# Half-by-half down and output projections, and staggered retention chunks, in a one-core decoder layer kernel

## The reference

```python
def _macaron_layer(x, mixer, f1g, f1u, f1d, ln1g, ln1b, ln2g, ln2b, f2g, f2u, f2d, ln3g, ln3b):
    x = _layernorm(ALPHA * x + 0.5 * _swiglu(x, f1g, f1u, f1d), ln1g, ln1b)
    m, st = mixer(x)
    x = _layernorm(ALPHA * x + m, ln2g, ln2b)
    x = _layernorm(ALPHA * x + 0.5 * _swiglu(x, f2g, f2u, f2d), ln3g, ln3b)
    return x, st
```

```python
    inner = jnp.einsum('bnhd,bmhd->bhnm', q, k) * decay[None]
    intra = jnp.einsum('bhnm,bmhe->bnhe', inner, v)
    cross = jnp.einsum('bnhd,bhde->bnhe', q, sp) * xi[None, :, :, None]
    s_new = jnp.exp(L * lg)[None, :, None, None] * sp + jnp.einsum('bmhd,bmhe->bhde', k * zeta[None, :, :, None], v)
```

## Time and profile before

| what | value |
|---|---|
| median of 3 runs | 1487.87 us (1487.46 to 1488.2) |
| the profiled execution's own time | 1489.0 us |
| its span, first to last instruction | 1487.3 us |
| mean granted TensorE clock | 0.972 of full |
| TensorE busy | 1405.3 us (94% of the span) |
| VectorE, ScalarE, GpSimd busy | 556.1, 417.2, 193.6 us |
| HBM read, written | 169.00 MB, 7.02 MB |

### The profile page before, as it was taken

The page is one execution under the profiler, slowest core; times in us unless marked ns, Lnnn a source line. Parts: engine busy times, 40 slices in busy tenths (PEclk is TensorE's granted clock), DMA queues, the critical chain, the costliest instruction groups (busy, mean ns, idle before and its releaser), DMA issues. The chain is left out here.

```text
span 1487.3 us, 27099 instructions
## 1 busy us (share of the span) xinstructions
PE 1405.3 (94%) x10150; PEld 1216.6 (82%) x10150; DVE 556.1 (37%) x1102; ACT 417.2 (28%) x622; POOL 193.6 (13%) x309
## 2 busy tenths in 40 slices
PE   6999999999999999999997768999899999999995
PEld 6999999999987647777773445567699999999994
DVE  3332323322251338893112446452533333322224
ACT  4333333212241231100131001340734343322223
POOL 0000000033213102212113212102500000000011
PEclk9999999999999989999998978999999999999998
DMA  5222222233322328888365744501022222223221
GB/s 190 84 86 84 85 85 84 68 115 106 94 67 75 103 73 261 261 267 265 133 220 188 244 149 170 194 6 57 29 85 85 85 86 93 89 68 90 87 80 60
DMA packets 65352, 176.76 MB, mean 119 GB/s; under 512 B 9681, under 2 KB 13778, under 8 KB 65042
## 3 DMA queue, kind: packets, MB, share of 16 engines
q1 hardware_dynamic: 49874, 131.30, 27.1%
q0 software_dynamic: 14560, 40.96, 8.4%
q10 hardware_dynamic: 864, 3.80, 0.7%
HBM read 169.00 MB, written 7.02 MB: 118 GB/s over the span
## 5 line engine op out<-in xcount | busy, mean ns | idle before, releaser
L365 PE MATMUL ps<-x_high,w_high 128*128 128x280 f32 (+1 forms) x1408 | 413.9, 294 | 17.8 <-DVE x_low L1078 10.6
L365 PE MATMUL ps<-x_high,w_low 128*128 128x280 f32 (+1 forms) x1408 | 411.0, 292 | 0.0
L365 PE MATMUL ps<-x_low,w_high 128*128 128x280 f32 (+1 forms) x1408 | 410.9, 292 | 0.0
L1072 DVE TENSOR_TENSOR w_low<-wring,w_high 128x1024 fp32r<-128x1024 f32 (+1 forms) x136 | 163.0, 1199 | 508.5 <-ACT w_high L839 508.4
L365 PEld LDWEIGHTS ps<-x_high,w_high 128*128 128x128 f32 x1408 | 267.9, 190 | 22.8 <-issue 13.6
L365 PEld LDWEIGHTS ps<-x_low,w_high 128*128 128x128 f32 x1408 | 268.0, 190 | 0.0
L365 PEld LDWEIGHTS ps<-x_high,w_low 128*128 128x128 f32 x1408 | 267.4, 190 | 0.0
L365 PE MATMUL ps<-xbuf,wring 128*128 128x280 f32 x1056 | 262.6, 405 | 1.2 <-ACT aux L839 0.9
L839 ACT ACTIVATE w_high<-wring 128x1024 fp32r<-128x1024 f32 (+1 forms) x136 | 140.7, 1035 | 423.7 <-PE ps L365 422.7
L365 PEld LDWEIGHTS ps<-xbuf,wring 128*128 128x128 f32 x1056 | 197.5, 191 | 58.3 <-issue 9.2
L365 PE MATMUL ps<-h_high,w_low 128*128 128x280 f32 (+1 forms) x704 | 203.8, 289 | 0.0
(11 more groups left out here) (190 smaller groups left out, 1184.5 us busy)
## 6 DMA issues: line engine op xcount, KB each, us to landing
wring<-in_wg SPq DMA_DIRECT2D x44, 512.0 KB, 3.4
wring<-in_wu SPq DMA_DIRECT2D x44, 512.0 KB, 3.4
wring<-in_w_in SPq DMA_DIRECT2D x33, 512.0 KB, 4.1
wring<-in_wd SPq DMA_DIRECT2D x32, 512.0 KB, 3.5
dring<-in_k_pool POOLq DMA_DIRECT2D x64, 256.0 KB, 4.5
dring<-in_k_pool SPq DMA_DIRECT2D x64, 256.0 KB, 3.9
dring<-in_v_pool POOLq DMA_DIRECT2D x64, 256.0 KB, 4.3
dring<-in_v_pool SPq DMA_DIRECT2D x64, 256.0 KB, 3.9
```

Of the source, the lines that this page charges most:

```text
L365: return nc.tensor.matmul(out, lhs, rhs, start=start, stop=stop, **kw)
L1072: v.tensor_tensor(wl[:, to, 0:n], w4[:, s, 0:n], wh[:, to, 0:n].bitcast(F32), ALU.subtract) \
```

## The change

1. The down projections of both SwiGLUs run over all 8 output tiles for column half 0, and then once more over all 8 for half 1. The weights of the down projection are loaded and split twice. Half 0's norm is spread over the second pass; half 1's norm comes in the next stage (for n = 0 between the first tiles of the input projection) or at the end (n = 2). For half 0 of n = 0 and 2 POOL makes the whole sum of the tiles and the sum of the squares, so that TensorE has one matmul for each; half 1 is as before, with ScalarE's squares.
2. The output projection goes the same way, half 0 for all tiles and then half 1, and the second SwiGLU's first tile takes turns with norm 1 of half 1. VectorE writes the full value (`gained`), ScalarE only the rounded one.
3. Retention: the inner products of chunk t + 1 are made ahead of the turned output of chunk t - 1, and the output bank alternates between 2 and 6.
4. The sample states' decay goes to POOL, and the stores of the new states behind all eight of these.
5. The loads of `cst` and `acc` move, to behind ScalarE's x_high and to POOL behind norm 0.

```diff
-FF_W = [FT // 2 + KT] * 3 + [FT // 2]
+FF_W = [FT // 2 + 2 * KT] * 3 + [FT // 2]
...
+        def summed(n, a):
+
+            return n != 1 and a == 0
...
-                for s in range(3):
-                    down_chunk(s, wds[m][0])
-                with loop(sp, KT - 1, [(f, 1) for f in free[:3]]) as i:
-                    for s in range(3):
-                        down_chunk(s, wds[m][bass.ds(i + 1, 1)].rearrange("a p n -> (a p) n"))
+                for a in range(2):
+                    with loop(sp, KT, [(f, 1) for f in free[:3]]) as i:
+                        for s in range(3):
+                            down_chunk(s, wds[m][bass.ds(i, 1)].rearrange("a p n -> (a p) n"))
...
+                def down(a, j):
+                    pe.wait_ge(sem("r_done"), rdone.up())
+                    for s in range(3):
+                        if s == 2:
+                            pe.wait_ge(sem("hl_done"), FT * (m + 1))
+                        pe.wait_ge(sem("wl_done"), wl_done.up())
+                        wide_split(m, j, (j + s) % 2, hh, hl, 8 * s, DOWN[s] // P, FT, parts=(a,)).then_inc(sem(f"w_free{s}"), 1)
+
                 with loop(pe, KT // 2, [(wl_done, 6), (rdone, 2)]):
                     for j in range(2):
-                        pe.wait_ge(sem("r_done"), rdone.up())
...
-                norm(2 * m)
...
+                        down(0, j)
+                down(1, 0)
+                norm_mean(2 * m, 0)
+                down(1, 1)
+                down(1, 0)
+                down(1, 1)
+                norm_var(2 * m, 0)
+                with loop(pe, KT // 4, [(wl_done, 6), (rdone, 2)]):
+                    for j in range(2):
+                        down(1, j)
+
+            def norm_mean(n, a):
+                m = int(n > 0)
                 if n == 0:
                     pe.wait_ge(sem("cst_in"), 16)
-                pe.wait_ge(sem("sum_done"), (KT - 2) * (n + 1))
+                pe.wait_ge(sem("sum_done"), sum_at(2 * n + a + 1))
+                last = mm(ps[:, 4 + a, 0:HW[m]], c("mean"), rsum_t[:, cols(a, m)], True, summed(n, a))
+                if not summed(n, a):
+                    pe.wait_ge(sem("r_done"), 2 + KT * (2 * n + a + 1))
+                    last = mm(ps[:, 4 + a, 0:HW[m]], c("mean"), rs[n][:, KT - 1, cols(a, m)], False, True)
+                last.then_inc(sem("mean_full"), 1)
+
+            def norm_var(n, a):
...
+                if summed(n, a):
+                    pe.wait_ge(sem("sq_done"), sq_at(2 * n) + 1)
+                    mm(ps[:, 6 + a, 0:HW[m]], c("mean"), squares(3, m)).then_inc(sem("sq_free"), 1)
+                    return
...
@@ -461,6 +501,10 @@
                     if a:
                         last.then_inc(sem(f"w_free{t}"), 1)
+                    elif t == 0:
+                        norm_mean(0, 1)
+                    elif t == 1:
+                        norm_var(0, 1)
...
+            ret_in(real(0), P)
             for t in TILES:
-                ret_in(real(t), P)
                 value_pages(1)
                 pe.wait_ge(sem("it_done"), t + 1)
                 pe.wait_ge(sem("qx_done"), t + 1)
                 pe.wait_ge(sem("sr_done"), t + 1)
                 for hd in range(RH):
-                    o = ps[:, 2, hd * P:(hd + 1) * P]
+                    o = ps[:, 2 + 4 * (t % 2), hd * P:(hd + 1) * P]
...
                 new_state(t + 1, P, vr[:, t, :])
-                value_pages(1)
-                ret_out(t)
-                pe.wait_ge(sem("mixr_done"), t + 1)
+                if t < 3:
+                    ret_in(real(t + 1), P)
+                    value_pages(1)
+                if t:
+                    ret_out(t - 1)
+            ret_out(3)
+            pe.wait_ge(sem("mixr_done"), 4)
...
-            for d in range(KT):
-                pe.wait_ge(sem("r_done"), KT + 1 + d + 1)
-                for a in range(2):
+            for a in range(2):
+                for d in range(KT):
+                    pe.wait_ge(sem("r_done"), KT * (2 + a) + d + 1)
...
+                    if a:
+                        if d == 0:
+                            norm_mean(1, 0)
+                        elif d == 3:
+                            norm_var(1, 0)
             ffn(1)
+            for part in (norm_mean, norm_var):
+                part(2, 1)
...
@@ ScalarE @@
-            act.dma_start(cst[:, :], consts).then_inc(sem("cst_in"), 16)
-            act.dma_start(acc[:, :], acc_tab).then_inc(sem("acc_in"), 16)
...
+                for d in range(KT):
+                    output(1, d % 2, d < KT - 1)
+                    if d == 3:
+                        norm_std(2 * m, 0)
+                    if d in (5, 6):
+                        norm_out(2 * m, 0, range(4 * (d - 5), 4 * (d - 4)))
...
+            act.dma_start(cst[:, :], consts).then_inc(sem("cst_in"), 16)
             weight_high(1, 1)
             ffn(0)
+            norm_squares(0, 1)
+            norm_std(0, 1)
+            norm_out(0, 1)
...
@@ VectorE @@
+                for d in range(KT):
+                    output(1, d, d % 2, d < KT - 1)
+                    if d == 0:
+                        center(2 * m, 0)
+                    elif d == 3:
+                        inverse(2 * m, 0)
+                    elif d == 4:
+                        normal(2 * m, 0)
...
+            chunk_scale(0)
             for t in TILES:
...
                 v.tensor_tensor(sr, sr, ps[:, 3, :], ALU.add).then_inc(sem("sr_done"), 1)
-                group_norm(t, P, lambda hd: ps[:, 2, hd * P:(hd + 1) * P])
-                gated(t, real(t), P, 5)
+                if t < 3:
+                    chunk_scale(t + 1)
+                group_stats(P, out_ps)
+                if t:
+                    gated(t - 1, real(t - 1), P, 5)
+                group_norm(t, P, out_ps)
+            gated(3, real(3), P, 5)
...
-                seq(v.tensor_tensor(h4(o, P), h4(o, P), gam[:, 8:12].unsqueeze(2).broadcast_to([P, RH, P]), ALU.mult))
+                dve.wait_ge(sem("st_aged"), b + 1)
...
+            for d in range(4, KT):
+                mixed(1, d)
+                normal(1, 0, range(2 * d - 8, 2 * d - 6))
+                for k in range(2 * d - 8, 2 * d - 6):
+                    gained(0, k)
+            center(1, 1)
+            inverse(1, 1)
+            for d in range(0, KT, 2):
+                normal(1, 1, range(d, d + 2))
+                for k in range(d, d + 2):
+                    gained(1, k)
...
@@ GpSimd @@
+            def norm_squares(n):
...
+                for d in range(KT):
+                    pool.wait_ge(sem("c_done"), 2 * KT * n + d + 1)
+                    o, part = squares(3, m), squares(d % 3, m)
+                    pool.tensor_tensor(part if d else o, r[:, d, cols(0, m)], r[:, d, cols(0, m)], ALU.mult)                         .then_inc(sem("sq_part"), 1)
+                    if d:
+                        pool.wait_ge(sem("sq_part"), (2 * KT - 2) * (n // 2) + 2 * d)
+                        pool.tensor_tensor(o, o, part, ALU.add).then_inc(sem("sq_done" if d == KT - 1 else "sq_part"), 1)
...
             index_pages(pool, 0)
             index_pages(pool, 1)
-            norm(0)
+            norm_sums(0, 0)
+            norm_squares(0)
+            norm_sums(0, 1)
+            pool.wait_ge(sem("sq_free"), 4 + sq_at(2))
+            pool.dma_start(acc[:, :], acc_tab).then_inc(sem("acc_in"), 16)
             index_pages(pool, 2)
...
             for b in range(NB):
+                pool.wait_ge(sem("cross_full"), b + 1)
+                o = st_ap(b).rearrange("p (h m) -> p h m", h=RH)
+                pool.tensor_tensor(o, o, c("gam")[:, 8:12].unsqueeze(2).broadcast_to([P, RH, P]), ALU.mult) \
+                    .then_inc(sem("st_aged"), 1)
+            for b in range(NB):
                 pool.wait_ge(sem("st_new"), b + 1)
```

More of the change, by code:

```diff
@@ L152, in live, with squares, sq_at, sum_at @@
             return slice(AT0[m], T)
[L154 to L158, removed]
+        def squares(d, m):
+            return acc[:, (d % 4) * HALF:(d % 4) * HALF + HW[m]]
+        def summed(n, a):
+            return n != 1 and a == 0
+        def sq_at(i):
+            return sum(1 if summed(*divmod(j, 2)) else KT for j in range(i))
+        def sum_at(i):
+            return sum(KT - 1 if summed(*divmod(j, 2)) else KT - 2 for j in range(i))
         ident = c("ident")
@@ L864, in output @@
                             weight_high(nxt, (j + s) % 2, DOWN[nxt])
-                    if more:
-                        ev(halves(s_buf[:, j, live(m)]), pair(j, m), scale=0.5).then_inc(sem("y_done"), 1)
-                    else:
-                        for a in range(2):
-                            ev(s_buf[:, j, cols(a, m)], ps[:, 2 * j + a, 0:HW[m]], scale=0.5).then_inc(sem("y_done"), 1)
+                    ev(s_buf[:, j, cols(a, m)], ps[:, 2 * j + a, 0:HW[m]], scale=0.5).then_inc(sem("y_done"), 1)
                 hdone = Tally(sem("h_done"), 2 + FT * m)
@@ L876, in ffn @@
```

(27 more changed lines are left out.)

243 lines of the change are left out of this document (129 added, 114 removed).

## The result

The changed kernel takes 1509.73 us (median of 4 runs, 1507.58 to 1513.28), the kernel before 1487.66 beside it (1485.24 to 1488.2). The ratio is 1.0158, with a 95% interval of 1.0141 to 1.0174: the kernel is 22 us slower, where 4.5 us slower had been forecast. The profiled execution of after took 1513.28 us, with a span of 1510.4 us.

The account below looks back on a forecast made before the run. TensorE, busy 94% of the span, was taken as the bound. Terms 24.9 + 1.5 + 12.6 + 0.6 - 7.1 - 8.5 - 5.5 - 14.0 = +4.5 us on 1487.9 gave 1492.4 us, range 1477 to 1503.

Parts of the forecast that it names:

- Down projection, the weight ring: Down projections: slot reload and split takes 6.0 us, so TensorE idles 0.6 us (m=0) or 0.75 (m=1) each pass.
- What is put into the second pass: Down projections, second pass: VectorE's and ScalarE's norm work mostly replaces ring stalls, costing 0.5 us; TensorE's norm matmuls 0.47 each.
- three for m = 1: Second down projection: TensorE has three norm matmuls there, 1.4 us.
- POOL: First down projection: POOL's sums follow its index page DMAs, so TensorE's mean waits 15.1 us, from 370.6 to 385.7.
- Norm 0 and norm 2: After the first down projection and at the kernel's end: only half 1's norm remains, gaining 7.1 and 8.5 us.
- Norm 1: Between output projection and second SwiGLU: 66.1 us become 59.2, POOL being the limit; gain 5.5 us after a clock deduction.
- term of the clock: Norm 1: 1.4 us taken off the gain for products at half clock, as TensorE idles between them.
- Retention: Retention chunks: the period falls from 13.9 to 9.2 us as a chunk's norm runs beside the next chunk; gain 14.0 us.
- Start: Kernel start: the load of `cst` takes ScalarE 0.57 us ahead of a high part TensorE waits for; +0.6 us.
- Retention is bound by its pages: Retention rival: pages land late, TensorE waits, and 12 us a chunk loses 8.4 of the gain; 1500.8 us, chance 0.15.
- The clock falls with the small stalls: Down projection rival: each of 21 stalls brings half clock and costs 1.3 us, 27 in all; 1520 us, chance 0.07.
- POOL is on time: First down projection rival: POOL's page loop ends by 365, saving 16.6 us; 1475.8 us, chance 0.06.

Follow-up runs that it names:

- the fifth experiment: Changed kernel with down slots loaded once VectorE has split them, POOL's second page loop behind half 0's norm work, and chunks of 8, 7 and 7 weight tiles: 1468.93 us.
- third experiment: Changed kernel with POOL's second index page loop moved behind the first half's sums and squares: 1496.94 us, ratio 1.0071 to the kernel before.
- The eighth experiment: Changed kernel with early down loads and POOL's second page loop moved back, plus norm 1's x made by ScalarE instead of VectorE: 1473.33 us.
- The ninth: As The eighth experiment, plus TensorE's mean of norm 1's second half ahead of the last two of eight product groups: 1474.36 us.
- first experiment: Kernel before with only the staggered retention chunks and two output banks: 1471.15 us, ratio 0.9918.
- tenth: Changed kernel with early loads, POOL's pages behind, chunks of 8, 7 and 7, norm 1's gains on ScalarE and its second mean earlier: 1465.26 us.

## Why the prediction was wrong, step by step

**Down projection, the weight ring (failed in size).** The mechanism was right, and the sum for the turn-round, 6.0 us, nearly so: in the chain after it is 6.15 (the load 3.6, the parts 1.09 and 1.28 with their hand-overs, and 0.16 from the last product to the next load, where 0.04 had been taken). The step that failed is the length of the pass that was added to it, "a chunk of 8 weight tiles ... 3.1 us" (3.0 in the second). That is the time of a chunk in an unbroken stream. A chunk that starts on an idle engine and must be complete before its slot is free takes 3.27 us in the chain (3.35 for m = 0). The evictions of half 0 lie 9.40 us apart in F (1349.09 to 1414.87 for seven) and 9.72 in A (302.11 to 379.85 for eight; the median landing there is 3.7). The stall is so 1.1 us instead of 0.75 in F and 1.2 instead of 0.6 in A. Over 15 stalls in F that is 6 of the 8.1 us that the forecast missed there. The other 2 lie in half 1, where the passes with VectorE's blocks take 9.9 to 10.4 us. In A it shows only behind the mean: from there to the last eviction were 68.9 us (388.3 to 457.2), where the terms had made 66.1.

**What is put into the second pass (a little too low).** "0.5 us more for the three places together": where the ring no longer stalls, in the fifth experiment, TensorE's idle time is 1.7 us in A and 2.3 in F. The 1.4 us of "three for m = 1" was too much: the traces have two of these matmuls in F, 0.9 us, and the third behind the last product.

**POOL (right).** The forecast wait of 15.1 us after 370.6 was 11.1 us up to 388.3. TensorE came 6.5 us later, by the ring and the start. The sums ended 2.4 later: POOL's list began 1.4 later, and each sum took 0.9 us with its wait instead of 0.77. To move one line in POOL's list gave the wait back (third experiment).

**Norm 0 and norm 2 (right).** -7.1 and -7.9 against -7.1 and -8.5. (The terms for norm 2, 27.2 less 18.4, make -8.8; the sum used -8.5.)

**Norm 1 (wrong in sign).** The forecast was 59.2 + 1.4 us, a gain of 5.5; measured are 68.0, a loss of 1.9. The chain of after has the last low part of the first half, TensorE's products up to the mean, and the same of the second half:

```profile
1056.28 0.88 POOL x_low L1604
...
1057.20 3.60 PE ps L373 x10
...
1069.38 1.55 POOL x_low L1604
...
1070.98 8.13 PE ps L373 x48
```

Three terms were too small. The first is POOL's part. Its eight low parts and two sums were to begin near 31 us behind the first product and to end at 38.9. The first low part began at 33.3, and the last ended at 42.6 (1056.28 + 0.88 - 1014.58). POOL's timeline shows what it waited for:

```profile
1047.86 0.87 POOL L1604 TENSOR_TENSOR x_low<-xbuf,x_high 128x272 fp32r<-128x272 f32 x1 [0.71 <-DVE xbuf L1218]
```

VectorE works without a gap from 1045.74 to 1056.5, and the chain runs along it there. So VectorE's list, which the change lengthened by 16 gains, sets the pace, and the forecast doesn't have it at all; it had called POOL the limit. The operations also take longer beside each other: POOL's 0.95 us each, where 0.8 was taken, and VectorE's 0.58 to 0.69, where a product of this kind alone takes 0.36 from start to start (tail of after, 2.91 us for 8). Behind the last low part TensorE still had 3.6 us of products at half clock ahead of the mean, where 0.9 had been allowed. And the last low parts and products took 9.7 us (1069.38 to 1079.11), not 7.1. The eighth experiment, which takes the gains out of VectorE's list, shows the first of these for 2.7 us. The ninth got 0.8 us from the order of the mean. The rest of the excess was read from the timeline but not tried alone.

**E (not in the forecast).** After D's last wait TensorE starts at a granted clock of 0.75 over 1082 to 1095, where before it ran on at 1.00 from 1074 to 1087: +2.1 us. The kernels with other clocks in E's first 13 us fit this: 252.9 us at 1.00 (first experiment), 254.4 at 0.87 (eighth), 255.3 at 0.80 (tenth), 255.6 at 0.75. The forecast had put its term of the clock into D.

**Retention (right, near its better bound, in part by luck).** The forecast period was 9.2 us, between VectorE's 7.4 and TensorE's 10.1. Measured are (886.75 - 864.59) / 3 = 7.4 us. The doubt about TensorE's 10.1, counted at a low clock, was justified, and it should have weighed more. But that the period equals VectorE's 7.4 is chance: the last two chunks lie only 6.0 apart, and it is TensorE, at a granted clock of 1.00, that is busy for 93% of these 27 us. By the prediction's own sum a period of 7.4 gives -19.4 us; the first experiment won 17.4, and where the 2 us are was not sought.

**Start.** +1.4 us in after, but kernels with the same code at the start show 288.5 to 290.1: no effect can be told from this spread.

**The rivals.** "Retention is bound by its pages": no, 17.4 us were won. "The clock falls with the small stalls": no. The windows above show 1.00 in both down projections, although each pass stalls. The Trainium skill (TensorE: Matmul & The Clock Gate, "A second HAM failure mode: psum-queue depth-cycling") says of one kernel that frequent small idles between groups of matmuls make the clock swing. The traces here don't bear this out for one idle of 0.5 to 1.0 us in every pass of 9.4 to 9.7 us; behind the wait of 11 us the clock did fall. "POOL is on time": no.

In sum: the errors of +3.9 in A, +8.1 in F, +7.4 in D and +2.1 in E make 21.5 us, less 4.3 in C; +0.8 at the start and +0.6 in G bring it to 18.6, the difference between +4.5 and +23.1.

## What to carry to other kernels

When a buffer's reuse distance is halved, write its whole turn as one chain, with the first and last products at their time from idle, not at the rate of an unbroken stream, and count every kind of buffer in the ring: here the raw slots were the first limit and the two buffers for split parts stood right behind it. A slot should be released by its last reader, which was VectorE and not TensorE. A value that is needed earlier than before must be followed into the list of each engine that makes it; one line moved in POOL's list was worth 12 us.

## What was not expected of the hardware

VectorE's and POOL's operations on SBUF (the on-chip memory that both read) take longer beside each other. In the kernel with chunks of 8, 7 and 7 a low part of 1024 columns takes 1.79 us beside POOL's sums, and 1.22 to 1.23 us in the passes next to it:

```profile
339.18 1.79 DVE L1151 TENSOR_TENSOR w_low<-wring,w_high 128x1024 fp32r<-128x1024 f32 x1 [1.80 <-ACT w_high L904]
```

```profile
338.17 3.45 POOL L1595 TENSOR_TENSOR scr<-scr,rbuf 128x280 f32<-128x280 f32 x3
```

The Trainium skill (SBUF — State Buffer, "SBUF: two separate sides") says that a VectorE operation with two SBUF inputs and a GpSimd operation that reads SBUF exclude each other for the length of an instruction. The longer times of both engines here agree with that in kind; how long each is held up, no run here shows.

The landing of these loads is far from proportional to their bytes: 512 KB 3.6 us, 384 KB 3.3, 256 KB 2.7, 192 KB 2.4.
